# Gathers from bf16 parts, and one w2 unit of the last pair loaded ahead, in a hybrid decoder step on one Trainium2 core

## What is computed

```python
def moe_ffn(xf, router_w, router_b, w1, b1, w2, b2):
    logits = (xf @ router_w).astype(jnp.float32) + router_b.astype(jnp.float32)
    top_val, top_idx = lax.top_k(logits, TOP_K)
    gates = jax.nn.softmax(top_val, axis=-1)
...
        hcat = xb @ w1[e] + b1[e]
        x_glu = jnp.minimum(hcat[:, ::2], SWIGLU_LIMIT)
        x_lin = jnp.clip(hcat[:, 1::2], -SWIGLU_LIMIT, SWIGLU_LIMIT)
        g = x_glu * jax.nn.sigmoid(SWIGLU_ALPHA * x_glu) * (x_lin + 1.0)
        return g @ w2[e] + b2[e]
...
```

## Time and profile before

| what | us |
|---|---|
| median of the runs | 1233.53 |
| the profiled execution, its own time | 1233.13 |
| its span, first to last instruction | 1230.2 |
| TensorE busy in the span | 1191.4 (97%) |
| VectorE, ScalarE, GpSimd busy | 360.1, 242.6, 55.2 |

### The profile page before, as it was taken

One profiled execution on the slowest core, in us unless ns is written; L12 is line 12 of the kernel. 1 busy time (PEld: TensorE's weight loads), 2 busy tenths in 40 slices (PEclk: granted clock), 3 DMA queues, 4 the chain that ended last, 5 costly groups with the idle time before them and its releaser, 6 DMA issues.

```text
span 1230.2 us, 14774 instructions
## 1 busy us (share of the span) xinstructions
PE 1191.4 (97%) x5852; PEld 522.2 (42%) x5852; DVE 360.1 (29%) x746; ACT 242.6 (20%) x489; POOL 55.2 (4%) x49
## 2 busy tenths in 40 slices
PE   9999999899999999999999999999999999999997
PEld 6777666535333333333333333333333333333332
DVE  2467336765312130312212120303122121212122
ACT  2013453627010201111111201011111111110113
POOL 0000033520000000000000000000000000000000
PEclk9999999999999999999999999999999999999999
DMA  9677657479899999999999999999999999999995
GB/s 293 208 252 255 205 188 285 139 266 416 348 414 429 429 426 429 429 428 428 429 429 427 428 429 429 427 428 429 428 427 429 429 428 427 429 429 427 427 429 240
DMA packets 64367, 463.56 MB, mean 377 GB/s; under 512 B 7704, under 2 KB 25268, under 8 KB 38380
## 3 DMA queue, kind: packets, MB, share of 16 engines
q1 hardware_dynamic: 62206, 459.02, 90.9%
q10 hardware_dynamic: 1582, 2.22, 0.5%
q0 software_dynamic: 544, 1.84, 0.4%
HBM read 455.82 MB, written 7.24 MB: 376 GB/s over the span
## 4 chain that ended last, share of the span: by engine, by line
PE 76%; DMA 19%; DVE 2%; issue 1%; ACT 1%; SPq 0%; DVEq 0%; ACTq 0%
PE ps L2408 28%; DMA ring<-in_w 19%; PE ps L2432 12%; PE ps L1883 10%; PE ps L2344 5%; PE ps L2328 2%; PE ps L2336 2%; PE ps L2297 2%; PE ps L2330 1%; PE ps L2394 1%; PE ps L2168 1%; PE ps L2416 1%; PE ps L1925 1%; PE ps L1959 1%; PE ps L2352 1%
## 5 line engine op out<-in xcount | busy, mean ns | idle before, releaser
L2408 PE MATMUL ps<-ring,own 128*64 128x512 f32 x1456 | 324.1, 593 | 6.8 <-DMA ring<-in_w 6.8
L2408 PEld LDWEIGHTS ps<-ring,own 128*64 128x64 f32 x1456 | 110.8, 137 | 199.4 <-issue 178.9
L1745 DVE TENSOR_SCALAR own<-ps 128x512 f32<-128x512 f32 x32 | 22.1, 691 | 526.5 <-PE ps L2408 526.5
L2432 PE MATMUL ps<-ring,own 128*64 128x512 f32 x592 | 133.5, 595 | 5.4 <-issue 5.2
L2408 PE MATMUL ps<-own 128*64 128x512 f32 x592 | 133.9, 593 | 3.0 <-DMA own<-in_w 3.0
L1883 PE MATMUL ps<-own,ring 128*128 128x288 f32 x512 | 129.9, 409 | 0.0
L1883 PEld LDWEIGHTS ps<-own,ring 128*128 128x128 f32 x512 | 95.1, 190 | 28.8 <-issue 4.4
L2432 PE MATMUL ps<-own 128*64 128x512 f32 x432 | 98.4, 595 | 3.5 <-issue 2.6
L2344 PE MATMUL ps<-own 128*128 128x512 f32 x180 | 88.5, 617 | 0.0
L2432 PEld LDWEIGHTS ps<-ring,own 128*64 128x64 f32 x592 | 44.2, 137 | 84.4 <-issue 75.7
L2408 PEld LDWEIGHTS ps<-own 128*64 128x64 f32 x592 | 44.5, 137 | 83.4 <-issue 80.5
(11 more groups left out here) (381 smaller groups left out, 973.2 us busy)
## 6 DMA issues: line engine op xcount, KB each, us to landing
ring<-in_w SPq DMA_DIRECT2D x128, 2048.0 KB, 31.1
own<-in_w SPq DMA_DIRECT2D x63, 2048.0 KB, 29.6
ring<-in_w_in SPq DMA_DIRECT2D x16, 1024.0 KB, 7.6
ring<-in_cache_win_k SPq DMA_DIRECT2D x8, 1024.0 KB, 5.4
ring<-in_cache_win_v SPq DMA_DIRECT2D x8, 1024.0 KB, 5.0
ring<-in_w_out SPq DMA_DIRECT2D x6, 1024.0 KB, 10.9
ring<-in_state_ssm SPq DMA_DIRECT2D x8, 512.0 KB, 7.3
out_ssm_sample<-ring SPq DMA_DIRECT2D x8, 512.0 KB, 8.9
```

The lines of the kernel that those rows point to most:

```text
L1745: nc.vector.tensor_scalar(xg_o, hid[:, 0], LIMIT, None, ALU.min).then_inc(sem("glu_ready"), 1)
L2408: last = nc.tensor.matmul(ps[C * half:C * half + C, 1 + m, :], xT[:, k, C * u:C * u + C], rows[:, D * half + 512 * m:D * half + 512 * m + ...
L2432: last = nc.tensor.matmul(ps[C * half:C * half + C, 4, :], gT[:, (k % 4) * P + C * (k // 4):(k % 4) * P + C * (k // 4) + C], rows[:, 512 * ...
```

## The change

It has four parts.

1. **The gather** reads bf16. Each of the two prompt tiles of xn is split into three bf16 parts (`token_parts`), the samples use stacked parts as the first pair does (`sample_parts`), and VectorE writes the selections S1 in bf16 (`S1b`, and `S1s` on 96 rows). The gather has 2 x 7 instructions in the program where it had 2 x 3, which ran as two float32 passes each. ScalarE and VectorE make the parts once, ahead of the first pair.
2. **One w2 unit of the last pair**, n = 8, is loaded ahead as eight pieces of 512 columns, 256 KB each, into rooms (`kept`) that are dead by then, and stays there. SP issues six of them after the load of n = 7 of the first pair, once `xT_ps` is at 2 and `S_ready` at 5; ScalarE issues two after the last rounding. In the last pair the loads of n = 9 to 11 move up by one room (`end_unit`), and `second` waits for `kept_in` instead.
3. **norm_final** is loaded by ScalarE at the start of the closing turn instead of by GpSimd at the start of the loop, since its place now lies in xn.
4. To make room, the gated units are written in place (`gg = xl`), so VectorE waits for `gT_ps` ahead of its second clamp; some constants and small regions move, and the squares of the last norm go elsewhere.

```diff
+            act.wait_ge(sem("xT_ps"), 2)
+            rounded(sample_parts[0:96], first_parts[0:96], 8, 0)
+            for c in range(2):
+                rounded(token_parts[c][0], xn[:, c, :], 9 + c, 0)
+            for c in range(2):
+                rounded(token_parts[c][1], xn[:, c, :], 11 + 2 * c, 4)
+                rounded(token_parts[c][2], xn[:, c, :], 12 + 2 * c, 5 + c)
+            act.wait_ge(sem("xn_ready"), XN_PARTS)
+            for i in range(KEPT - 2, KEPT):
+                act.dma_start(kept[i], a["w2"][0][NE - 2].rearrange("(s p o) c -> s p (o c)", p=P, o=W2_ROWS)[0][:, 512 * i:512 * i + 512]).then_inc(sem("kept_in"), 16)
...
                 unit_load(2 * (n // PER_PAIR), n)
+                if n == UNITS - 2:
+                    sp.wait_ge(sem("xT_ps"), 2)
+                    sp.wait_ge(sem("S_ready"), HEAD_SELECTIONS)
+                    for i in range(KEPT - 2):
+                        sp.dma_start(kept[i], w2[NE - 2, 0][:, 512 * i:512 * i + 512]).then_inc(sem("kept_in"), 16)
...
             for n in range(PER_PAIR):
-                wait_used(n, more * MORE_TURNS + FIRST_TURNS)
+                if n == KEPT_UNIT:
+                    continue
+                m = end_unit(n)
+                of, which, j = pair_unit(n)
+                src = (w1 if which == "w1" else w2)[NE - 2 + of, j]
+                wait_used(m, more * MORE_TURNS + FIRST_TURNS)
                 if n < PER_PAIR - 1:
-                    unit_load(NE - 2, n)
+                    sp.dma_start(unit(m % UNITS), src).then_inc(unit_full(m % UNITS), 16)
...
-            pool.wait_ge(sem("expert_slot_used"), RING)
-            pool.dma_start(nfin, a["norm_final"].partition_broadcast(P)).then_inc(sem("b1_in"), 16)
...
             def closing_turn(pt):
 
+                act.dma_start(nfin, a["norm_final"].partition_broadcast(P)).then_inc(sem("small_w_in"), 16)
                 act.wait_ge(sem("turned_ps"), 2)
...
                 nc.vector.tensor_scalar(xg_o, hid[:, 0], LIMIT, None, ALU.min).then_inc(sem("glu_ready"), 1)
+                dve.wait_ge(sem("gT_ps"), et + 1)
                 nc.vector.tensor_scalar(xl_o, hid[:, 1], -LIMIT, LIMIT, ALU.max, ALU.min).then_inc(sem("hid_read"), 1)
...
+            for r in range(1, 3):
+                last = nc.vector.tensor_copy(posm[NS * r:NS * r + NS, 2, :], posm[0:NS, 2, :])
+            link(last)
+            for c in range(2):
+                left_over(xn[:, c, :], token_parts[c][0], 10 + c)
+            for c in range(2):
+                dve.wait_ge(sem("xn_left"), 3 + c)
+                left_over(xn[:, c, :], token_parts[c][1], 12 + 2 * c)
...
             def gather():
 
+                pe.wait_ge(sem("xn_ready"), XN_PARTS)
                 for half in range(2):
-                    for c in range(3):
-                        n = ROWS[c]
-                        last = nc.tensor.matmul(ps[:, 6 + half, :], S1[0:n, c, :], xn[0:n, c, 512 * half:512 * half + 512], start=(c == 0), stop=(c == 2))
-                    last.then_inc(sem("gather_ps"), 1)
+                    columns = slice(512 * half, 512 * half + 512)
+                    for c in range(2):
+                        for part in range(3):
+                            nc.tensor.matmul(ps[:, 6 + half, :], S1b[:, c, :], token_parts[c][part][:, columns], start=(c == 0 and part == 0), stop=False)
+                    nc.tensor.matmul(ps[:, 6 + half, :], S1s[0:96], sample_parts[0:96, columns], start=False, stop=True).then_inc(sem("gather_ps"), 1)
```

More of the change, by code:

```diff
@@ L104, in shape_constants @@
     put("ones", np.ones((P, P)))
+    put("slot", np.tile(r % C + 1, (P, 1)))
+    s = np.arange(NS)
+    same = (s[:, None] // DT) == (s[None, :] // DT)
+    put("expert", np.tile(np.arange(NE), (P, 1)))
+    put("expert_row", (r[:, None] % NE) == (np.arange(NE + 2) % NE)[None, :])
+    put("thresholds", np.tile(C * np.arange(1, MAX_PASS, PASS_STEP), (P, 1)))
+    first_dead = pos
     put("le", r[:, None] <= r[None, :])
@@ L321, in hymba_step @@
         r_Xs = take(G * N)
+        r_small = take(160)
         ident = const("ident")
@@ L352, in hymba_step @@
         w_dt_at = used[0]
+        assert at_Bcw - at_spare == 4 * SLOT + 256 and w_dt_at - at_Bcw == 1116
         r_dt = take(KT * H)
@@ L359, in hymba_step @@
         stat = take(64)
+        at_dts = used[0]
+        dts = take(6 * 48)
+        rows_small = take(128 + 80)
         st4 = take(32)
-        dts = take(6 * 48)
-        r_small = take(160)
-        rows_small = take(128 + 80)
         spare.append(take(2 * SLOT))
@@ L436, in hymba_step @@
         rt = sub(r_xbcP, 2656, 892)
-        xg, xl, sg, gg = (sub(r_xbcT, i * 512, 512) for i in range(4))
-        nfin = sub(r_xbcT, 2048, D)
-        b1p = sub(r_Bcw, 0, F2 // 2).bitcast(BF16)
+        gate_at = at_xbcP + 3624
+        xg, xl, sg, unused = (own[:, gate_at + 512 * i:gate_at + 512 * (i + 1)] for i in range(4))
+        gg = xl
+        squared = own[:, gate_at:gate_at + D]
+        parts_more = [own[:, gate_at + 2048 + 512 * i:gate_at + 2048 + 512 * (i + 1)].bitcast(BF16) for i in range(3)]
+        assert gate_at + 2048 + 3 * 512 <= at_spare
+        sample_parts = parts_more[0]
+        xn_bf = [sub(r_xn, 512 * i, 512).bitcast(BF16) for i in range(6)]
+        token_parts = [[parts_more[1], xn_bf[4], xn_bf[5]], [parts_more[2], xn_bf[0], xn_bf[1]]]
+        S1b = d3(sub(r_xbcP, 256, 2 * C).bitcast(BF16), 2 * C)
+        S1bs = S1s.unsqueeze(1)
+        nfin = sub(r_xn, 0, D)
+        b1p = own[:, at_Bcw - 256:at_Bcw - 256 + F2 // 2].bitcast(BF16)
+        dead_at, dead = CONST_AT["dead"]
+        assert dead + G * N + 160 >= 1024 and consts.shape[1] == dead_at + dead
+        KEPT = 8
+        free_at = dead_at + dead + G * N + 160 - 1024
+        kept = [own[:, free_at:free_at + 512], own[:, free_at + 512:free_at + 1024], own[:, at_dts:at_dts + 512],
+                own[:, at_Bcw + 3 * G * N:at_Bcw + 3 * G * N + 512], unused, own[:, at_xnT + 2048:at_xnT + 2560],
+                sub(r_xn, D, 512), sub(r_xn, D + 512, 512)]
+        assert at_xnT + KT * TOK == at_xbcP
         b1s = sub(r_xn, 0, F2)
@@ L542, in h_bank @@
             return 6 if c == 2 else 2 + 2 * c + half
+        XN_PARTS = 15
         FIRST_BANKS, LATER_BANKS = (6, 7), (3, 5)
@@ L2425, in second @@
                         n = first + 2 * W1_UNITS + W2_UNITS * u + k // W2_ROWS
-                        if k % W2_ROWS == 0:
-                            wait_unit(n)
+                        here = ending and n == KEPT_UNIT
+                        m = end_unit(n) if ending else n
+                        if here:
+                            pe.wait_ge(sem("kept_in"), 16 * KEPT)
+                        elif k % W2_ROWS == 0:
+                            wait_unit(m)
                         if ending and n == PER_PAIR - 1 and k % W2_ROWS == 2:
                             pe.wait_ge(sem("end_rows"), 16)
-                        rows = d3(unit(n % UNITS), D)[:, k % W2_ROWS]
+                        rows = None if here else d3(unit(m % UNITS), D)[:, k % W2_ROWS]
                         for half in range(2):
                             last = nc.tensor.matmul(ps[C * half:C * half + C, 4, :], gT[:, (k % 4) * P + C * (k // 4):(k % 4) * P + C * (k // 4) + C],
-                                                    rows[:, 512 * half:512 * half + 512], start=(k == 0), stop=(k == KT - 1))
+                                                    kept[2 * k + half] if here else rows[:, 512 * half:512 * half + 512], start=(k == 0), stop=(k == KT - 1))
                         if k % 2 == 1:
```

40 lines of the change are left out of this document (20 added, 20 removed).

## The result

The changed kernel takes 1237.66 us (median of 19 runs, 1234.53 to 1242.31), against 1233.71 us of the kernel before (19 runs, 1231.96 to 1235.42): 1.0031 of its time, 95% interval 1.0022 to 1.0040. The forecast was 1234.7 us and no change that could be told; it is slower, and 0.3 us outside the range on the slow side. The profiled execution took 1237.66 us with a span of 1235.5.

What follows compares the result with a forecast made beforehand. The loop was taken as bound by the DMA queue. Delays of 0.8 + 1.2 + 1.2 - 0.7 = 2.5 us, less 0.3 of slack and 0.97 gained, gave +1.2 on 1233.53: 1234.7 us, range 1232.6 to 1237.4.

Steps and rivals of the forecast that it cites:

- The bound: Whole loop: the DMA queue bounds it at 58.8 us a pair, so TensorE's savings before the last pair return as waiting.
- The gather: Ahead of the first w2 unit of each pair: 14 bf16 instructions take 3.1 us instead of 5.90.
- Preparing the parts: ScalarE and VectorE from 311.3 us on: some 12 us of roundings and subtractions, hidden, cost nothing.
- The gain at the end, 0.97: Last pair on TensorE: the wait for unit 8 goes, 0.97 us gained; the other waits cost nothing.
- The pause, 0.8 of 3.9: Queue's standstill near 312 us: six pieces take 3.9 us, mostly hidden, so the stream starts 0.8 us later.
- The prediction's own sign: Queue after the pause: a rate of 400 GB/s or so from 313 us would show the forecast right.
- ScalarE's two transfers, 1.2 each: Full queue near 323 and 1165 us: two pieces and norm_final each cost the stream 1.2 us.
- What comes back, 0.7: First pair: the shorter gather frees slots sooner, giving back 0.7 us of 1.0 us lost stream.
- The sum: Unit 7 of the last pair lands 2.5 us later; TensorE is delayed 2.2, saves 0.97: +1.2 us.
- The pieces collide with the stream: Rival at SP's queue, 312 us: stream starts up to 3.9 us late, giving 1237.8 us; chance 0.18.
- The end follows the last landing: Rival at the end: one unit less in the queue gains 2.4 us, giving 1231.1 us; chance 0.08.
- TensorE's clock falls: Rival in the loop: 5.5 us of waiting a pair drops the clock to 1.2 GHz, giving 1249 us; chance 0.04.

Runs made afterwards that it cites:

- x_instream: Changed kernel with SP's six pieces issued two loads later, behind the load of n = 10 of the first pair: 1238.07 us, 1.0030 of the kernel before.
- x_late: Changed kernel with norm_final issued by ScalarE behind the last sums instead of at the start of the closing turn: 1234.83 us, 1.0010 of the kernel before.
- b_nfin: Kernel before, float32 gather kept, with only norm_final issued by ScalarE at the start of the closing turn: 1235.30 us, 1.0014 of the kernel before.
- the two last runs: Changed kernel without the kept unit and with norm_final issued behind the last sums, measured twice: 1232.54 us (0.9985) and 1233.01 us (0.9993).

## Why the prediction was wrong, step by step

- **The bound.** Right. The loop follows the queue at 58.75 us a pair, TensorE is busy for 275.07 of 300 us from 800 to 1100 (91.7%; "near 91%"), and the work that the fifteen gathers save on TensorE (42 us in the forecast) brought nothing through the pairs.

```profile
800.00:1100.00 300.00, 275.07 (x1253) 97.88 (x1255) 58.10 (x95) 38.63 (x62) 0.00 (x0) 1.00 1.01 428
```

- **The gather.** Right: from its first instruction to the first of w2 behind it 350.43 - 347.53 = 2.90 us, forecast 3.1 for the group, against 5.90 in the earlier trace rows (timeline of TensorE, which has a record of 13 of the 14 instructions).

```profile
347.53 1.24 PE L2406 MATMUL ps<-own 128*128 128x512 bf16 x5
348.61 0.38 PE L2407 MATMUL ps<-own 96*128 96x512 bf16 x1
348.83 1.46 PE L2406 MATMUL ps<-own 128*128 128x512 bf16 x6
350.12 0.38 PE L2407 MATMUL ps<-own 96*128 96x512 bf16 x1
350.43 3.65 PE L2498 MATMUL ps<-own 128*64 128x512 f32 x16
```

- **Preparing the parts.** Right that it costs nothing: no wait appears at the gather.
- **The gain at the end, 0.97.** Right in kind: units 7, 8 and 9 follow without a wait for unit 8 or 9. Against the version that has the early norm_final but no kept unit the gain is larger, 1.33 us, since unit 8 is waited for longer there. The openings' wait for VectorE's copy, priced at nothing, took 0.21 us.
- **The pause, 0.8 of 3.9. This is the step that failed.** Everything up to the first packet was right: issues from 312.05 (312.1) and the first packet at 315.30 - 2.30 = 313.0 (312.9). What was wrong is the sentence "The stretch that stores the same 2 KB rows ran at 405 GB/s, so they take 3.9 us, to 316.8". They ran until 323.51 - 2.30 = 321.2, from 318.4 on beside the first packets of unit 9, and the stream stood 3.0 us behind. The prediction's own sign, 400 GB/s or so from 313 us, failed: 243 and 269 came. The row that I took the earlier trace rows showed stores in a queue that was running; the pieces are loads, and they start a queue that stood still. The text had the nearer row, 216 GB/s in the first 1.9 us behind the pause, and let it move the answer by 0.5 us. Had the pieces been priced at 216, six would have taken 1.57/0.216 = 7.3 us, from 312.9 to 320.2. The stream's effective start was 316.5, so this gives 3.7 us of delay, nearer to the 3.0 than the 0.8 that I took. But those 216 belong to 16 KB rows whose rate rose right behind them (421 from 320 us on), and to price all six pieces at them is hindsight. The row of the same kind stood in the trace of the kernel before and was not looked for: four loads of 256 KB with 2 KB rows, from standstill, 232 GB/s over 4 us (under x_instream). At that rate six pieces take 1.57/0.232 = 6.8 us, from 312.9 to 319.7, and the stream starts 3.2 us late.
- **ScalarE's two transfers, 1.2 each.** Right: 1.4 and 1.3 us. The rule of the Trainium skill, "DMA: Bandwidth & Descriptors", section "Issuing engines are not separate DMA queues", that transfers of different engines share the same 16 DMA engines, agrees with these steps and with x_late.
- **What comes back, 0.7.** Somewhat small: 1.0 to 1.1 us, at the upper bound. By b_nfin and the two last runs it comes with the gather.
- **The sum.** Unit 7 at +4.6 instead of +2.5; with the 0.3 us of slack and the 0.97 of gain the same working gives +3.4, and the trace +3.0 (packet and instruction records shift against each other by some tenths within an execution). The other three terms came out about 0.2 and 0.1 over the forecast and 0.35 under it; that they cancel and leave the pause alone is luck.
- **The rivals.** *The pieces collide with the stream* happened, at its place, SP's queue at 312 us, and past its deciding point of 2.1; at 3.0 its formula gives 1234.7 + 2.2 = 1236.9, between the two medians 1236.44 and 1237.66. It had 0.18, for the reason that VectorE's product and its predecessors would be in time; they were, and it did not matter. *The end follows the last landing* did not: unit 8's bytes left the queue and the end came later. *TensorE's clock falls* through the waits of the loop did not either, the clock in it is 1.00 above. The Trainium skill, "TensorE: Matmul & The Clock Gate", section "HAM oscillation — how this bites in real kernels", tells of a kernel whose waits for DMA lowered the clock; with the waits of these loops, 1.9 us at most, no profile's loop here shows it.

## What to carry to other kernels

A gap in a queue is not worth its length times the full rate: price what is put into it by rows of the same kind: loads with loads, of the same size, from a queue in the same state. Such rows can stand in another part of the same trace, as those of line 614 did. Moving a transfer out of a full queue pays only if it is put where the bytes are really free, here behind unit 7 of the last pair (norm_final, 1.4 us), and not where they push a stream that nothing later catches up. A saving on an engine that waits for a queue can still pay through the slots that it frees earlier (1.1 us here), even if its own 42 us don't show.

## What was not expected of the hardware

- The same six loads of 2 KB rows moved at 243 to 269 GB/s (the result's profile) at the start of a queue that had stood still, and at 355 GB/s in the running stream; 59 to 81 of their 768 packets took over 150 ns in the first case, in five profiles with three layouts of the source, and 20 in the second. Four loads of 256 KB in the kernel before did the same (232 and 408 GB/s), and one load of 1 MB from standstill was at 403 in its third us. Why several small loads start so slowly is open: the layout is at most a small part of it, and whether the kept unit in fewer and larger loads would be hidden wasn't tried.
- The granted clock falls to 0.50 at one or two places ahead of the loop (near 12, 206 and 230 us) in some executions of the same program and in others not. Heads of profiles without a fall ahead of them lie within 0.4 us of the kernel before, with one fall 0.65 to 1.19 late, and with two 2.01 to 2.87. What decides it in an execution, these runs don't show.
